# Two-layer decoder trunk: products of zeros ahead of x, moved waits, memory turns and head copy, and an earlier round count

## What is computed

```
for i in range(2):
    h = x @ w_in            # queries, keys, values, memory queries
    mix = swa_sink_attention(...)   if i == 0      # 12 heads, window 128, a sink per head
          rms_norm(diff_attention(...)) if i == 1  # 6 heads of 128, two softmaxes each
    mem_out = softmax(q_mem km^T) vm               # 4 heads over 256 memory tokens
    x = layer_norm(alpha * x + concat(mix, mem_out) @ w_out[i])
    f = moe_ffn(x)          # 64 experts, 8 chosen per token in groups, and a shared one
    x = layer_norm(alpha * x + f)
```

## Time and profile before

| what | value |
|---|---|
| median of 3 runs (lowest, highest) | 1222.53 us (1222.42, 1223.16) |
| profiled execution, its own time | 1226.36 us |
| span of the profiled execution | 1224.6 us |
| TensorE busy | 1165.0 us (95%) |
| moved by DMA | 446.92 MB, mean 365 GB/s |
| first instruction of SP and ScalarE's queue | 0.81 us |
| ScalarE: issue of the sinks' load | 2.22 us, takes 4.35 |
| ScalarE: its first table load, then first copy of x | 6.60 us, takes 1.28; 7.90 us, takes 0.60 |

### The profile page before, as it was taken

One profiled execution on the slowest core, in us unless ns is written; L12 is line 12 of the kernel. 1 busy time (PEld: TensorE's weight loads), 2 busy tenths in 40 slices (PEclk: granted clock), 3 DMA queues, 4 the chain that ended last, 5 costly groups with the idle time before them and its releaser, 6 DMA issues.

```text
span 1224.6 us, 22651 instructions
## 1 busy us (share of the span) xinstructions
PE 1165.0 (95%) x8928; PEld 709.3 (58%) x8930; DVE 349.2 (29%) x903; ACT 303.3 (25%) x712; POOL 64.8 (5%) x103
## 2 busy tenths in 40 slices
PE   7999999999989999998999999999999899999985
PEld 6774855555555555554677648555555555555552
DVE  0333712122222212221523456121222222222214
ACT  1453312222121212221223432121222222122212
POOL 1332000000001000000012100000000010000000
PEclk9999999999999999999999999999999999999998
DMA  9842799999999999999990468999999999999994
GB/s 361 330 168 108 298 384 420 420 421 422 422 422 421 411 420 421 421 421 421 388 357 14 156 241 348 382 420 420 421 422 421 422 410 395 402 420 423 420 421 181
DMA packets 74502, 446.92 MB, mean 365 GB/s; under 512 B 6976, under 2 KB 12480, under 8 KB 24896
## 3 DMA queue, kind: packets, MB, share of 16 engines
q1 hardware_dynamic: 72208, 441.22, 88.4%
q10 hardware_dynamic: 2224, 4.72, 1.0%
HBM read 444.86 MB, written 1.05 MB: 364 GB/s over the span
## 4 chain that ended last, share of the span: by engine, by line
PE 66%; DMA 22%; issue 6%; DVE 2%; POOL 1%; ACT 1%; SPq 1%; DVEq 0%; POOLq 0%; ACTq 0%
DMA ring<-in_w_up 22%; PE bank L1228 15%; PE bank L1209 12%; PE bank L1262 12%; PE bank L741 6%; PE bank L760 4%; PE bank L799 4%; PE bank L1270 4%; PE bank L1085 2%; PE bank L1235 1%; POOL soft L707 1%; PE bank L775 1%; PE bank L1108 1%; PE bank L730 1%; DVE work L1631 1%
## 5 line engine op out<-in xcount | busy, mean ns | idle before, releaser
L1228 PE MATMUL bank<-ring,work 128*64 128x256 f32 x1952 | 225.4, 380 | 15.8 <-DMA ring<-in_w_up 15.8
L1209 PE MATMUL bank<-ring,work 128*64 128x256 f32 x1984 | 227.8, 382 | 9.7 <-DMA ring<-in_w_gate 9.4
L1262 PE MATMUL bank<-ring,work 128*32 128x512 f32 x1904 | 222.0, 595 | 1.5 <-issue 1.4
L1209 PEld LDWEIGHTS bank<-ring,work 128*64 128x64 f32 x1984 | 142.2, 137 | 116.9 <-issue 58.9
L1228 PEld LDWEIGHTS bank<-ring,work 128*64 128x64 f32 x1952 | 147.8, 137 | 84.1 <-issue 23.6
L1922 DVE SCALAR_TENSOR_TENSOR yhalf<-bank,gcol,yhalf 128x512 fp32r<-128x512 f32 x124 | 93.1, 751 | 215.9 <-ACT yhalf L1550 215.9
L1914 DVE TENSOR_TENSOR work<-work,bank 128x256 f32<-128x256 f32 x64 | 26.9, 421 | 370.5 <-PE bank L1228 370.5
L1550 ACT ACTIVATE yhalf<-bank,gcol 128x512 fp32r<-128x512 f32 x124 | 85.2, 687 | 182.7 <-PE bank L1262 182.7
L1262 PEld LDWEIGHTS bank<-ring,work 128*32 128x32 f32 x1904 | 57.4, 109 | 118.2 <-issue 111.2
L1392 ACT ACTIVATE work<-bank 128x512 f32<-128x512 f32 (+4 forms) x177 | 77.9, 440 | 103.0 <-PE bank L741 46.2
L1392 ACT ACTIVATE back<-bank 128x128 fp32r<-128x128 bf16 x64 | 17.7, 277 | 283.4 <-PE bank L1181 283.4
(11 more groups left out here) (187 smaller groups left out, 846.9 us busy)
## 6 DMA issues: line engine op xcount, KB each, us to landing
ring<-in_w_gate SPq DMA_DIRECT2D x124, 1024.0 KB, 14.7
ring<-in_w_up SPq DMA_DIRECT2D x122, 1024.0 KB, 16.3
ring<-in_w_down SPq DMA_DIRECT2D x119, 1024.0 KB, 15.4
ring<-in_w_in_b SPq DMA_DIRECT2D x3, 3072.0 KB, 18.6
ring<-in_w_out SPq DMA_DIRECT2D x4, 2048.0 KB, 13.3
home<-in_w_gate SPq DMA_DIRECT2D x4, 1024.0 KB, 18.0
ring<-in_w_down SPq DMA_DIRECT2D x8, 512.0 KB, 13.9
ring<-in_w_in_a ACTq DMA_DIRECT2D x1, 3072.0 KB, 19.6
```

Of the source, the lines that this page charges most:

```text
L1209: last = pe.matmul(gate_bank[slots_of(e), 0:HID], xg[:, k, slots_of(2 * j + e)], w[e][:, k, :], start=(k == 0), stop=(k == KT - 1))
L1228: last = pe.matmul(up_bank[slots_of(e), 0:HID], xg[:, k, slots_of(2 * j + e)], w[e][:, k, :], start=(k == 0), stop=(k == KT - 1))
L1262: last = pe.matmul(yb[half][rows_of(t, e), :], hT[b][:, f, slots_of(e, t)], w[e][:, f, half * 512:half * 512 + 512], start=(f == 0), stop= ...
```

## The change

It makes seven moves. (1) VectorE sets `zeros` as its first instruction and GpSimd no longer does. (2) TensorE multiplies zeros into bank 7: eight products before x's first half is waited for, three between the halves, seven after the second. (3) ScalarE computes one exponential of a zero before it issues the load of the sinks. (4) The waits for k0, k1, v, q0 (layer 0) and km, vm, qm (layer 1) go from ahead of filler 0 into the first `scores`. (5) The last of the memory turns goes from filler 5 to filler 6, the products of qm are split 8 and 8 over fillers 6 and 7, where they were 2, 7 and 7 over fillers 5 to 7, and ScalarE's copies follow. (6) VectorE copies the first four turned heads after eight scaled tiles, where it was after eleven. (7) `one_hot8` goes behind the count of rounds, and VectorE reads the count right behind it, ahead of the gates.

```diff
-        CONSTS = 16
+        CONSTS = 15
+        WARM = (8, 3, 7)
@@ gpsimd
-            step(pool.memset(zeros[:], 0.0))
@@ tensor
+            def warm(count):
+                for n in range(count):
+                    pe.matmul(banks[7][:], zeros[:, 0:P], zeros[:], start=True, stop=True)
+
+            pe.wait_ge(sem("zeros_set"), 1)
+            warm(WARM[0])
             pe.wait_ge(sem("const"), IDENT)
...
                     for t in range(TT):
+                        if t > 0:
+                            warm(WARM[1])
                         pe.wait_ge(sem(f"x_in{t}"), 16)
                         for half in range(2):
                             turn_rows(x, G[l, "x"] + 2 * t + half, t, half)
+                    warm(WARM[2])
                     for n in range(4):
                         evacuated(pe, G[l, "x"] + n)
...
                     tiles("q0", wq, 0, xT, 0, 16)
-                    for name in ("k0", "k1", "v", "q0"):
-                        evacuated(pe, G[0, name])
...
-                    for name in ("km", "vm", "qm"):
-                        evacuated(pe, G[1, name])
@@ filler_0
                     elif i == 5:
-                        for n in (1, 2, 3):
+                        for n in (1, 2):
                             turn_rows(memnat, G[0, "mem"] + n, n // 2, n % 2)
+                    elif i == 6:
+                        turn_rows(memnat, G[0, "mem"] + 3, 1, 1)
                         part_landed(pe, (0, "in1"), 1)
-                        tiles("qm", wm, 0, xT, 0, 2)
-                    elif i == 6:
-                        tiles("qm", wm, 0, xT, 2, 9)
+                        tiles("qm", wm, 0, xT, 0, 8)
                     elif i == 7:
-                        tiles("qm", wm, 0, xT, 9, 16)
+                        tiles("qm", wm, 0, xT, 8, 16)
@@ scores
+                    if pair[0] == 0:
+                        for name in (("k0", "k1", "v", "q0"), ("km", "vm", "qm"))[l]:
+                            evacuated(pe, G[l, name])
@@ scalar
+            act.wait_ge(sem("zeros_set"), 1)
+            act.activation(lamv[:, 7:8], zeros[:, 0:1], ACT.Exp)
             act.dma_start(sinkrow[:], sinks.broadcast_to([P, MIX_HEADS])).then_inc(sem("sinkrow"), 16)
...
-                        elif i == 5:
-                            for t in range(TT):
-                                take(copy, rows_out(memT, t, 1), "mem", 4, P, 2 * t + 1)
+                        elif i in (5, 6):
+                            take(copy, rows_out(memT, i - 5, 1), "mem", 4, P, 2 * (i - 5) + 1)
@@ vector
+            dve.memset(zeros[:], 0.0).then_inc(sem("zeros_set"), 1)
             for l in range(DEPTH):
...
                                                      op0=ALU.mult, op1=ALU.mult).then_inc(sem("heads_normed"), 1)
+                            if c == 7:
+                                take(copy, mixT[:, 0:2, :], "heads", 2, SEQ, 0)
                     norm_heads(HEADS_EARLY, 0)
-                    take(copy, mixT[:, 0:2, :], "heads", 2, SEQ, 0)
...
-                one_hot8(0, 0, 0)
                 link(dve.tensor_reduce(cmax[:], bank_at(g)[:, TT * NE:2 * TT * NE], AX_X, ALU.max))
...
                 dve.tensor_copy(nround_i[:, l:l + 1], nround[:]).then_inc(sem(f"routed_{l}"), 1)
+                one_hot8(0, 0, 0)
+                dve.wait_ge(sem(f"routed_{l}"), 1)
+                rounds = dve.value_load(nround_i[0:1, l:l + 1], min_val=0, max_val=3) + 1
                 link(dve.tensor_tensor(gate[:], aff[:], chosen[:], ALU.mult))
...
                 one_hot(0, 0, 0, 0)
-                dve.wait_ge(sem(f"routed_{l}"), 1)
-                rounds = dve.value_load(nround_i[0:1, l:l + 1], min_val=0, max_val=3) + 1
```

## The result

The changed kernel takes 1215.47 us (median of 5 runs, 1215.17 to 1217.13) against 1223.16 (5 runs, 1222.42 to 1223.46) for the one before, run beside it: ratio 0.9939, 95% interval 0.9927 to 0.9952, so 0.6% or 7.5 us faster (5.9 to 8.9). The forecast was 1217.2, range 1216.0 to 1220.5. The profiled execution took 1215.17 us, its span is 1213.2.

A forecast was written before the change was run, and what follows sets the result against it. Experts run at the weights' pace, so only TensorE gains ahead of them count: 1.9 + 0.89 + 0.84 + 0.65 + 0.8 + 0.2 = 5.3 us, taking 1222.53 to 1217.2. Range 1216.0 to 1220.5, stretched to include a late clock.

The forecast's parts named there:

- the clock did not rise late: Rival at the start: turns keep TensorE's clock low, k0 starts 2.5 us later, time 1220.2 us; chance 0.18.
- the weights did not set the end: Rival for the whole kernel: the weight stream is full all along, TensorE only waits longer, 1222.5 us; chance 0.08.
- zeros do lift the clock: Contradicts the slower rival at the start: zeros don't lift the clock, head long at half clock, up to 1232; chance 0.04.
- Start: TensorE's start: zero products raise the clock early, so k0 and k1 run faster; 1.9 us, bounds 1.4 to 2.3.
- 6.92 at full clock: Start: q0's 32 records take 6.92 us, taken as the full-clock time of k0 and k1, against 8.88.
- Start of k0: k0 waits for its weights, so its start at 10.44 us stays within 0.3; no gain counted.
- The faster turns give nothing themselves: Start: k0 can't start before its weights, so faster turns of x gain nothing; only k0 and k1 do.
- Waits of the first scores: Ahead of filler 0, both layers: waits of 0.89 and 0.84 us are covered by the filler; gain 1.73 us.
- Memory turns: Filler 5: 0.84 us wait removed, a new stall of 0.1 to 0.3 appears; 0.65 kept, bounds 0.4 and 0.84.
- Head copy: Layer 1's scaled heads: copying after eight tiles begins 0.8 us earlier and removes TensorE's 0.81 us wait; gain 0.8.
- Routing: Routing, both layers: count read 0.69 us sooner, but most lost to later waits; 0.2 us together, bounds -0.3 to 0.9.
- hidden under nothing: Routing: VectorE's moved reading of the count holds up the gates by 0.5 to 0.9 us, with nothing covering it.

The follow-up runs named there:

- no_zeros: The changed kernel with all three counts of zero products set to 0: 1219.47 us, ratio 0.9960 to the kernel before.
- route_only: The kernel before with the routing change alone (count ahead of `hot`, reading ahead of the gates): 1222.96 us against 1224.01, ratio 0.9991.
- again_2: Another execution of the changed kernel, nothing edited, one run: 1217.19 us.
- again_3: One more execution of the changed kernel, nothing edited, one run: 1216.82 us.
- load_last: The changed kernel with VectorE's reading of the count behind the gates again, the count still ahead of `hot`: 1217.45 us, ratio 0.9946 to the kernel before.
- after: The first profile of the changed kernel, nothing edited: 1215.17 us for that execution, median 1215.47.
- hot_first: The changed kernel with `hot` ahead of the count again, the reading still ahead of the gates: 1218.23 us, ratio 0.9953 to the kernel before.
- first_eight: The changed kernel with only the eight zero products ahead of x, without the three and the seven: 1218.38 us, ratio 0.9952 to the kernel before.
- old: The kernel before, run and profiled again with nothing edited: 1224.11 us, ratio 1.0000.
- waits_back: The changed kernel with the waits for the first scores ahead of filler 0 again in both layers: 1218.69 us, ratio 0.9954 to the kernel before.

## Why the prediction was low

The mechanism held: gains only ahead of the experts, one by one, kept to the end; the experts run as they did. Rival by rival: the clock did not rise late; the weights did not set the end; zeros do lift the clock. What failed is the size of four terms, which add 1.5 us to 5.3, and one that the sum left out, 0.2 more. The largest miss, the routing, is one of mechanism: an overlap that was denied.

- **Start**, forecast 1.9, measured 2.18, in the first pair of profiles 1.66. The step that failed took the kernel before at 8.88 from a single execution; over four it is 9.36, because the rise of its clock moves. With no_zeros (8.70) and route_only (8.72), which start as the kernel before does, the mean of six is 9.15 and the gain 1.97, so this term is known to some 0.2 only. "6.92 at full clock", taken from q0, was low by 0.3 for k0 and k1: 0.07 of it is the wait ahead of them, 0.15 lies where k1's records follow k0's (starts 0.31 and 0.27 apart, not 0.22) and 0.09 at the step to v. The two errors have opposite signs.
- **Start of k0**, left at nothing, measured 0.18, or 0.29 if one counts from the turns of x's second half, which came 0.1 later in the four profiles of the changed kernel. "The faster turns give nothing themselves" holds only where k0 stands for its weights; where x came late (again_2, again_3), k0 followed the second turns by 2.50 us where it had been 3.0. The scatter of the start itself (10.23 to 10.93 in all eight) is larger than the term. ScalarE's exponential, the later sinks and q0's weights cost nothing, as said.
- **Waits of the first scores**, forecast 1.73, measured 2.23. The step that failed took idle time as the whole price of a wait; what lies under the modelled end (0.16) and the slower first product behind the wait (0.07) come on top in each layer.
- **Memory turns**, forecast 0.65, measured 0.81. The new stall is there, at the place named, at 0.32, the top of the 0.1 to 0.3; the removed wait was again worth more than its idle time (1.10 for 0.84).
- **Head copy**, forecast 0.8, measured 0.79. Here nothing comes on top of the idle time, because the wait is shortened and not removed: the turns ahead end at 708.59 in the changed kernel, the products start at 708.62, and they take 3.70 in both. The idle time falls from 0.81 to 0.03, which is the gain.
- **Routing**, forecast 0.2, measured 0.78. The step that failed: "hidden under nothing". The reading does hold up the gates, by 0.35 in layer 0 (in layer 1 the gates start 0.10 behind `hot`), not by 0.74 and 0.47, since `hot` covers the rest. So the copy of gathered rows starts 2.62 behind the gather in layer 0, and the wait at the 25th record that was to eat the gain is missing; one of 0.22 at the ninth came instead. The wait at the 25th is what load_last shows.

Sum of the measured terms: 2.18 + 2.23 + 0.81 + 0.79 + 0.78 + 0.18 = 6.97, against 7.0 outside the experts. The subtraction of 3.83 for the slow first profile was right: these us lay in its experts (875.8 against 871.2 to 871.8). With 7.0 off, 1222.53 gives 1215.5, which is what was measured; the match to 0.1 is luck, since the kernel before took 1223.16 beside it, which would give 1216.2, and a repeat of the changed kernel took 1216.85. What failed is the gain: 7.0 by the marks, where the range ended at 6.5. The range missed since it bounded single terms from one execution each, and the idle rows as if they were whole prices; all the bounds' upper ends together gave 6.6.

What the trace still shows at these places in the changed kernel is small: 0.19 from the heads' turns to the products (0.03 of it idle), the stall of 0.32, and 0.22 at the gather's ninth record in layer 0. Together they are less than a median of a few runs tells here, and no version without them was run.

## What to carry to other kernels

Price a removed TensorE wait from start to start: the distance from the last record ahead of it to the second one behind it, against the same records in an unbroken stretch. Here that was 0.23 to 0.26 us more than the idle time shown. A wait that is only shortened gives the idle time and no more. A wait for something that another instruction could cover is moved together with that instruction or not at all; each half of such an edit can cost what the whole gains. Profile the kernel before more than once ahead of a sum over tenths of a us, since the clock's rise at the start (0.93 us) and a stage bound by transfers (4.6 us) move between executions.

## What the runs showed of the hardware

- Products of zeros lift TensorE's clock: eight of 128x512 in bf16, from 1.26 us on, and the turns at 4.76 take 1.14 us where they took 1.94 (after). The moment moves: in again_3 these turns take 1.50, in hot_first 1.94.
- The clock fell again behind them, during the second turns, after eight turns and a gap of 1.61 us, and stayed at 1.2 GHz into k0 (first_eight, granted clock 0.50 from 9 to 11).
- The granted clock reads 1.00 ahead of its first recorded change even where turns take 1.97 us instead of 1.15 (old; the earlier trace rows). Before that, durations are the only sign.
- In the kernel before, the rise moves between 13.8 and 15.6 us from execution to execution. The Trainium skill, "TensorE: Matmul & The Clock Gate", part 1, says that the rise varies from run to run by some 0.5 us to either side, as it isn't tied to the kernel's start. These four executions vary too, and by more: 0.9 to either side.
- VectorE's reading of a count into a register costs 0.96 us of idle time in layer 0 and 0.72 in layer 1 right behind the instruction that makes the count (hot_first), and only 0.35 and 0.10 with an instruction of 0.69 between (after).
- A TensorE record reads 0.38 us (128x256, fp32) where the next one starts 0.22 behind it, and the first record behind a wait holds its successor up for 0.29 (waits_back). So the idle time shown before a wait's end is 0.23 us less than what the wait costs.
